# Hybrid decoder layer on one core: alternating head products, adaLN operands swapped, the convolution's first tap on ACT, chunk order at the merge, the second norm shared with POOL

## The chip, the cores and the metric

One Trainium2 chip, one core of it. The metric is the device time of one launch in microseconds. The engines are TensorE (PE in the profile; PEld is its weight load), VectorE (DVE), ScalarE (ACT), GpSimd (POOL) and SyncE (SP, which only issues DMAs here).

## The reference

One layer for a prompt of 1024 tokens and 8 sample sequences of 4 tokens (1056 token columns together), model width 1024:

```
(s1, a1, g1, s2, a2, g2) = silu(c) @ w_ada + b_ada        # 9 conditioning vectors, 6 x 1024 outputs
h = RMSNorm(x) * (1 + a1) + s1
[q | k | v | hc | B | C | ga | gb] = h @ w_in
A: stick-breaking attention, 8 heads x 64, per-head QK RMSNorm, causal; samples also over 2048 cached keys
B: y = B * dwconv3_causal(C * hc)                          # 512 channels, taps w0, w1, w2 and a bias
mix = (sigmoid(ga) * (o_att @ w_att_out) + sigmoid(gb) * (y @ w_conv_out)) @ w_o
x = x + g1 * mix
x = x + g2 * sqrelu_mlp(RMSNorm(x) * (1 + a2) + s2)        # 1024 -> 4096 -> 1024
```

Outputs are the new x, the normalised keys, the values and the last convolution rows, for both groups. All is fp32.

## The kernel before

Tokens lie on the free axis, channels on the partitions. The 1056 columns are cut into 3 chunks of 352 (`c`), channels into blocks of 128 (`b`). Weights come as units of 128x1024 (`u`) through three buffers `raw`; POOL splits each unit into a high and a low fp32r part (`wh`, `wl`, two of each; L523, L525), and a dense product is three fp32r matmuls per 128 rows (hH.wh, hL.wh, hH.wl), 24 of them for one group (one unit, one chunk) into one PSUM bank. A split of unit u waits until the last group of unit u-2 is done, since it takes over its buffers.

The order is written by hand. Stages:

1. `first_units` (L620 to L650): for each of the 8 channel blocks two adaLN units (`ada`, L607: the weight unit is the operand held in the array, the 9 conditioning vectors pass it), then the first 6 groups of q and k advance by one block. DVE makes `mods` (L1060) and from them the block of h (L1072 to L1082).
2. q, k (head norms on ACT), v.
3. The mix, `for k in range(TICKS)`, 51 ticks, the same list on every engine. A tick holds one attention step: `scores` (512 keys or less by 128 queries, two heads), ACT's sigmoid, DVE's keep factors and scan (L1123, L1132), POOL's product (L550), and in the next tick `turn` (transposes, L701), DVE's copies AT (L1162, L1164) and `values` (L712). It also holds one or two dense groups (`DENSE_A`, and `DENSE_B` in the ticks with k % 8 in 0, 1, 3, 4, 6), one page item of the sample attention (L730, L741, L754), and in 32 of the ticks (k % 3 not 0) one adaLN unit. DVE's `convolve` (L1194) runs right after the last chunk of C has been multiplied by hc, ahead of that tick's `turned`.
4. Merge: o_att and y are split in high and low (`split_hi` on ACT, `split_lo` on DVE), then 24 pairs of half groups (ya, yb), block after block, each block in 3 chunks; DVE multiplies by the gates and adds, and makes mixH and mixL.
5. w_o, 24 groups, blocks 0 to 5 in 3 chunks each, then blocks 6 and 7 chunk by chunk. DVE adds to x (`add_wo`), ACT squares, and `rms2` (L802) sums the squares in the middle of the next group.
6. Second norm by chunk: ACT makes the inverse root, then for 8 blocks DVE scales (L1353), ACT makes h2H (L1006), DVE makes h2L (L1330).
7. MLP, 288 groups.

DVE, ACT and POOL each work strictly in program order, so what stands ahead of a waiting instruction holds all that follows.

Of the kernel before, what the change touches and what calls it, by code (L numbers as in the profile page):

```python
# [51 lines left out]
for _n, _w in (("ident", 128), ("headones", 128), ("scanmask", 513), ("trikeys", 128), ("newkeep", 66), ("newvalid", 256),  # L52
               ("selG", 16), ("headrow", 8)):
    TABLES[_n] = (_at, _at + _w)
    _at += _w
# [6 lines left out]
Group = namedtuple("Group", "kind u c bank eng at before")  # L62

# [8 lines left out]
class Plan:  # L72
# [42 lines left out]
    def build(self):  # L115
# [17 lines left out]
        for b in range(DB):  # L133
            for c in range(NCH):
                self.add("ya", self.merge0 + b, c, "d", b5)
                self.add("yb", self.merge0 + b, c, "d", b5)
        self.start("wo")
        for b in range(6):
            for c in range(NCH):
                self.add("wo", self.wo0 + b, c, "d", b5)  # L140
        for c in range(NCH):
            for b in (6, 7):
                self.add("wo", self.wo0 + b, c, "d", b5)
# [20 lines left out]

PLAN = Plan()
# [19 lines left out]
DENSE_A, DENSE_B, ITEM_AT, TURN_AT, ADA_AT = {}, {}, {}, {}, {}  # L185


def ticks():
    g, m, n = MIX0, 0, 16
    end = PLAN.phase["merge"][0]  # L190
    for k in range(TICKS):
# [13 lines left out]
        if k % 3 != 0 and n < 48:  # L205
            ADA_AT[k] = n
            n += 1
# [74 lines left out]
def program(nc, a):  # L282
    ctx = ExitStack()
    with ctx:
# [14 lines left out]
        cT = put("cT", [P, DB, 9], F32)  # L299
# [56 lines left out]
        h2L = inw("h2L", [P, DB, T], F32R, at=W + 4 * DB * T)  # L356
        top[0] = W + 8 * DB * T
# [14 lines left out]
        sz_ps, ada_ps, st_ps, o_ps = bank[2][:, 0:P], bank[3][:, 0:9], bank[4][:, 0:P], bank[6][:, 0:P]  # L372
# [6 lines left out]
        def tb(name, rows=P, lo=0, hi=None):  # L379
# [10 lines left out]
            csig c_ready squares rms_done rstd dense_done bank_dve bank_act dve_step act_step  # L390
# [5 lines left out]
            x1_done squares2 rms2_done rstd2 scaled2 h2_hi h2_lo hid_hi hid_lo y_ready y_out  # L396
# [17 lines left out]
        def _(sp):  # L414
# [59 lines left out]
            def load_x(b):  # L474
                sp.wait_ge(S["mix_lo"], NCH * (5 + b // 2))
                sp.dma_start(act8[:, b, :], a["xT"][:, b, :]).then_inc(S[f"x_in{b}"], 16)
# [26 lines left out]
        def _(pool):  # L503
# [8 lines left out]
            mark(pool.memset(ones[:, :], 1.0))  # L512
            pool.wait_ge(S["pool_step"], steps[0])
# [57 lines left out]
            for u in range(42, len(PLAN.where)):  # L571
                split(u)

        @block.tensor
        def _(pe):
# [62 lines left out]
            for kt in range(DB):  # L638
                for m in (kt, DB + kt):
                    if kt:  # L640
                        pe.wait_ge(S["mods_done"], ADA_NTH[m] - 1)
                    ada(m, bank[6 + m // DB][:, 0:9])
                if kt == 0:
                    pe.wait_ge(S["rstd"], NCH)
                    continue
                first_units(kt - 1)
# [30 lines left out]
            def scores(k):  # L677
                st = STEPS[k]
                for h in (0, 1):
# [5 lines left out]
                    if h == 1 and k - 1 in ADA_AT:  # L685
                        pe.wait_ge(S["mods_done"], ADA_NTH[ADA_AT[k - 1]] + 1)
# [17 lines left out]
            def values(k):  # L704
# [3 lines left out]
                for h in (0, 1):  # L708
                    pe.wait_ge(S["at_out"], 2 * k + h + 1)
                    head = slice((2 * st.p + h) * HD, (2 * st.p + h + 1) * HD)  # L710
# [3 lines left out]
                    mm.then_inc(S["av_done"], 1)  # L714
# [51 lines left out]
            for k in range(TICKS):  # L766
                if k < NSTEP:
                    scores(k)
                if k in DENSE_A:
                    dense(DENSE_A[k], hH, hL)  # L770
                if k in TURN_AT:
# [33 lines left out]
            pe.wait_ge(S["mix_lo"], NCH * DB)  # L805
            pe.wait_ge(S["s_o"], 2)
            for n in range(QK_N):
                dense(WO0 + n, mixH, mixL, halfway=(lambda n=n: rms2(n - 1)) if n else None)

            for g in range(MLP0, len(GROUPS)):  # L810
                if GROUPS[g].kind == "m1":
                    f, q, c = GROUPS[g].c
                    if f == 0:
                        pe.wait_ge(S["h2_lo"], DB * (c + 1) + (c == NCH - 1))
# [5 lines left out]
                          (lambda: rms2(QK_N - 1)) if g == MLP0 else None).then_inc(S["dense_done"], 1)  # L820
# [12 lines left out]
        def _(act):  # L833
# [11 lines left out]
            act.activation(cT[:, :, :].rearrange("p k c -> p (k c)"), sm("cT"), ACT.Sigmoid).then_inc(S["csig"], 1)  # L845
            act.preload_act_table_set("natural_log_exp_and_others")
            act.wait_ge(S["consts"], 1)
# [75 lines left out]
            spills = {}  # L923

            def evict(g, k):
# [5 lines left out]
                elif kind == "gate":  # L931
# [7 lines left out]
                    if c == NCH - 1:  # L939
                        spills[k + 1] = ("gate", n, g)  # L940
                elif kind == "B" and c == NCH - 1:
# [17 lines left out]
            for k in range(TICKS):  # L959
                if k < NSTEP:  # L960
                    probability(k)
                if k in spills:
                    spill(*spills[k])
                if k in DENSE_A:
# [5 lines left out]
                if k == NSTEP + 1:  # L970
                    split_hi(0)
# [3 lines left out]
            split_hi(1)  # L975
# [3 lines left out]
            for n in range(NCH * DB):  # L979
                b, c = n // NCH, n % NCH  # L980
# [11 lines left out]
            def inverse2(c):  # L992
                act.wait_ge(S["rms2_done"], 18 + 2 * c + 2)
# [4 lines left out]
            def second_hi(c):  # L998
                n = CH if c < 2 else LASTP
                if c == 2:  # L1000
                    act.wait_ge(S["scaled2"], 17)
                    act.activation(h2H[:, :, samp], hs2[:, :, :], ACT.Copy).then_inc(S["h2_hi"], 1)
                for b in range(DB):
                    x = DB * c + b
                    act.wait_ge(S["scaled2"], x + 1 + (c == 2))
                    act.activation(h2H[:, b, c * CH:c * CH + n], sc[x % 3][:, 0:n], ACT.Identity, bias=mods[:, 24 + b, 0:1])\  # L1006
                        .then_inc(S["h2_hi"], 1)

            for n in range(18):
                square2(n)  # L1010
            for c in range(NCH):
                square2(18 + 2 * c)
                square2(19 + 2 * c)
                inverse2(c)
                second_hi(c)
# [14 lines left out]
        def _(dve):  # L1030
# [21 lines left out]
            tt(cT[:, :, :], sm("cT").rearrange("p (k c) -> p k c", k=DB), cT[:, :, :], ALU.mult).then_inc(S["c_ready"], 1)  # L1052
# [3 lines left out]

            def modulation(m, ps):
                dve.wait_ge(S["ada_done"], ADA_NTH[m] + 1)
# [7 lines left out]
            for b in range(DB):  # L1066
                for m in (b, DB + b):
# [126 lines left out]
            def convolve(cb):  # L1194
# [4 lines left out]
                if cb:  # L1199
                    dve.wait_ge(S["spill1"], 16 * cb)  # L1200
                own()
                mark(cp(tail[:, cb, 0:2], up[:, 0:2]))
                last = cp(tail[:, cb, 2:18].rearrange("p (b j) -> p b j", j=2), us[:, :, 0:2])
                if cb == CB - 1:
                    last.then_inc(S["tail_ready"], 1)
                else:
                    mark(last)
                mark(ts(y, up[:, 2:SEQ + 2], w(0), sm("conv_b", cb, cb + 1), ALU.mult, ALU.add))
                mark(ts(ys, us[:, :, 2:6], w(0), sm("conv_b", cb, cb + 1), ALU.mult, ALU.add))
                own()  # L1210
                mark(stt(y, up[:, 1:SEQ + 1], w(1), y, ALU.mult, ALU.add))
                mark(stt(ys, us[:, :, 1:5], w(1), ys, ALU.mult, ALU.add))
                own()
                mark(stt(y, up[:, 0:SEQ], w(2), y, ALU.mult, ALU.add))
                mark(stt(ys, us[:, :, 0:4], w(2), ys, ALU.mult, ALU.add))

            def evict(g):
# [3 lines left out]
                if kind == "C":  # L1221
# [9 lines left out]
                    dve.wait_ge(S["bank_dve"], GROUPS[g].at)  # L1231
                    convolve(cb)
                elif kind == "B":
# [253 lines left out]
```

## Time and profile before

| | |
|---|---|
| median of 3 runs | 1870.39 us (1869.11 to 1870.75) |
| the profiled execution | 1871.02 us, its span 1869.2 us |
| PE busy | 1777.9 us, 95% of the span |
| DVE, POOL, ACT busy | 878.6, 659.8, 299.3 us |
| mean granted clock of TensorE | 0.966 |
| PE idle for DVE or ACT at the second norm's sums (L802) | 22.1 us |
| HBM traffic | 104 GB/s over the span |

The median of the runs and the profiled execution differ by 0.6 us. A matmul's own duration (about 320 ns for 352 columns) is longer than the distance to the next one, since they are pipelined; durations of a stretch are therefore read from start to start. The granted clock is a share of TensorE's 2.4 GHz: 1.00 or 0.50 (1.2 GHz) at any moment, in between only as a mean.

### The profile page before, as it was taken

To read this page: it belongs to the slowest core of one execution; us is meant where nothing else is said; L and a number is where in the kernel's file an instruction comes from. 1 tells how busy PE (TensorE), PEld (TensorE's weight loads), DVE (VectorE), ACT (ScalarE), POOL (GpSimd) and SP (SyncE) were. 2 spreads that over 40 slices of the span, in tenths; PEclk is the share of its full clock that TensorE was granted. 3 is DMA by queue.
4 is the path that set the end of the run, shared out by engine and by line. 5 is a ranking of instruction groups with operands and counts; after the bars stand their busy time and mean duration, and the time that the engine had idled before them with its cause. 6 is when DMAs were issued, how large, how long until landed. Compare 5 with 4: busy or idle time off the path is not lost. (4 is left out here: it accounts for less than half of the span.)

```text
span 1869.2 us, 29718 instructions
## 1 busy us (share of the span) xinstructions
PE 1777.9 (95%) x11934; PEld 1657.0 (89%) x11934; DVE 878.6 (47%) x1425; ACT 299.3 (16%) x583; POOL 659.8 (35%) x377
## 2 busy tenths in 40 slices
PE   7999998997989999999898969999999999999999
PEld 6989777776778887879898868999999999999999
DVE  1434155545444444432783246555454545455553
ACT  3123211010101111111210123201020202020200
POOL 1037034343424443442342213433333333333332
PEclk8699999998989999999999989999999999999999
DMA  6312064444544665643432101111111111111112
GB/s 218 118 55 79 35 223 165 155 161 137 196 144 156 227 205 183 212 150 127 186 138 93 45 23 35 46 46 46 46 48 53 47 46 46 46 46 46 46 46 93
DMA packets 72505, 196.83 MB, mean 105 GB/s; under 512 B 8081, under 2 KB 8210, under 8 KB 72370
## 3 DMA queue, kind: packets, MB, share of 16 engines
q1 hardware_dynamic: 67682, 179.76, 28.6%
q10 hardware_dynamic: 4688, 15.18, 2.1%
q8 instruction: 96, 1.57, 0.3%
q14 instruction: 39, 0.32, 0.0%
HBM read 175.41 MB, written 19.50 MB: 104 GB/s over the span
## 5 line engine op out<-in xcount | busy, mean ns | idle before, releaser
L523 POOL TENSOR_TENSOR wh<-raw,zero 128x1024 fp32r<-128x1024 f32 x116 | 220.0, 1897 | 789.0 <-PE bank L589 700.3
L525 POOL TENSOR_TENSOR wl<-raw,wh 128x1024 fp32r<-128x1024 f32 x116 | 285.2, 2458 | 9.1
L589 PE MATMUL bank<-hH,wh 128*128 128x352 f32 x816 | 280.5, 344 | 3.0 <-POOL wl L525 3.0
L589 PE MATMUL bank<-hL,wh 128*128 128x352 f32 x816 | 266.5, 327 | 0.0
L589 PE MATMUL bank<-hH,wl 128*128 128x352 f32 x816 | 266.0, 326 | 0.0
L589 PE MATMUL bank<-h2H,wh 128*128 128x352 f32 x768 | 248.4, 323 | 0.9 <-issue 0.9
L1303 DVE SCALAR_TENSOR_TENSOR act<-bank,mods,act 128x352 f32<-128x352 f32 (+1 forms) x216 | 122.3, 571 | 268.0 <-PE bank L589 262.0
L589 PE MATMUL bank<-hidH,wh 128*128 128x352 f32 x768 | 247.7, 323 | 0.0
L589 PE MATMUL bank<-h2H,wl 128*128 128x352 f32 x768 | 246.3, 321 | 0.0
L550 POOL TENSOR_TENSOR beta<-beta,kb 128x512 f32<-128x512 f32 (+3 forms) x96 | 122.5, 1296 | 350.9 <-DVE kb L1132 350.9
L589 PE MATMUL bank<-hidH,wl 128*128 128x352 f32 x768 | 246.3, 321 | 0.0
L589 PE MATMUL bank<-h2L,wh 128*128 128x352 f32 x768 | 246.1, 320 | 0.0
L589 PE MATMUL bank<-hidL,wh 128*128 128x352 f32 x768 | 246.1, 320 | 0.0
L589 PEld LDWEIGHTS bank<-hH,wh 128*128 128x128 f32 x816 | 156.9, 192 | 33.2 <-issue 25.8
L1371 DVE TENSOR_TENSOR rsq<-rel 128x352 f32<-128x352 f32 x96 | 92.1, 959 | 165.3 <-ACT rel L1024 165.3
L589 PEld LDWEIGHTS bank<-hH,wl 128*128 128x128 f32 x816 | 157.5, 193 | 1.8
L589 PEld LDWEIGHTS bank<-hL,wh 128*128 128x128 f32 x816 | 156.7, 192 | 0.0
L589 PEld LDWEIGHTS bank<-h2H,wh 128*128 128x128 f32 x768 | 144.3, 188 | 1.2 <-issue 1.1
L589 PEld LDWEIGHTS bank<-h2H,wl 128*128 128x128 f32 x768 | 144.6, 188 | 0.1
L589 PEld LDWEIGHTS bank<-hidH,wl 128*128 128x128 f32 x768 | 144.3, 188 | 0.0
L589 PEld LDWEIGHTS bank<-hidH,wh 128*128 128x128 f32 x768 | 144.1, 188 | 0.0
L589 PEld LDWEIGHTS bank<-h2L,wh 128*128 128x128 f32 x768 | 144.1, 188 | 0.0
(147 smaller groups left out, 2667.9 us busy)
## 6 DMA issues: line engine op xcount, KB each, us to landing
raw<-in_weights SPq DMA_DIRECT2D x168, 512.0 KB, 3.6
ring<-in_cache_k SPq DMA_DIRECT2D x128, 256.0 KB, 4.0
ring<-in_cache_v SPq DMA_DIRECT2D x128, 256.0 KB, 3.6
gate_scratch<-gt ACTq DMA_DIRECT2D x16, 528.0 KB, 3.7
act<-gate_scratch SPq DMA_DIRECT2D x16, 528.0 KB, 4.5
xt<-in_xT SPq DMA_DIRECT2D x8, 528.0 KB, 9.0
act<-in_xT SPq DMA_DIRECT2D x8, 528.0 KB, 4.5
out_yT<-act SPq DMA_DIRECT2D x8, 528.0 KB, 2.7
```

Source lines behind the costliest of these rows:

```text
L523: mark(pool.tensor_tensor(wh[u % 2][:, :], src[:, :], zero[:, 0:1].to_broadcast([P, 1024]), ALU.add))
L525: pool.tensor_tensor(wl[u % 2][:, :], src[:, :], wh[u % 2][:, :].bitcast(F32), ALU.subtract)\
L550: pool.tensor_tensor(b[:, 1:st.n + 1], b[:, 1:st.n + 1], kb[x % 4][:, 0:st.n], ALU.mult)\
L589: mm = pe.matmul(out, x, y, start=n == 0, stop=n == end)
L1303: one = stt(x, ps[:, 0:CH if c < 2 else LASTP], mods[:, col, 0:1], x, ALU.mult, ALU.add)
L1371: mark(tt(rsq[x % 2][:, :], rel[x % 2][:, :], rel[x % 2][:, :], ALU.mult))
```

## The change

- `values`: the products of the two heads of a step (each writes 64 partitions of the same bank) alternate, and both wait for the second head's AT.
- adaLN: the 9 vectors, padded to 32 columns, are held in a quarter of the array's columns (four quarters for 8 blocks of rows), and the weight unit passes them. The partial sums (4 x 32 rows x 128) go through a DVE copy `ada_y` and a second small product with `sel9`, which adds the quarters and turns the result. In the mix this turn stands one tick later; in stage 1 it stands behind the preceding block's 18 dense products.
- Convolution: tap 0 and bias go to ACT (`conv_first`); taps 1 and 2 stay on DVE but move to the first chunk of B, and where that is a `DENSE_A` group, behind `turned`.
- `split_hi` of chunks 0 and 1 one and two ticks earlier. The last two blocks of the merge go chunk by chunk, as do the first two of w_o, and the first w_o groups wait only for their own chunk of mixL.
- Second norm: of chunks 0 and 2, blocks 5 to 7 are scaled and subtracted on POOL, with two ACT operations each between; all of w_o's last four additions stand together ahead of chunk 1; the sums of groups 20 to 23 are taken later.

```diff
+MERGE_ORDER = by_blocks(range(6)) + by_chunks((6, 7))
+WO_ORDER = by_chunks((0, 1)) + by_blocks(range(2, 6)) + by_chunks((6, 7))
...
             def ada(m, out):
                 for kt in range(DB):
-                    mm = pe.matmul(out, raw[i % NRAW][:, kt * P:(kt + 1) * P], cT[:, kt, :], start=kt == 0, stop=kt == DB - 1)
+                    at = 32 * (kt % 4)
+                    mm = pe.matmul(out[at:at + 32, :], cT[:, kt, :], raw[i % NRAW][:, kt * P:(kt + 1) * P],
+                                   start=kt < 4, stop=kt >= 4, tile_position=(0, at))
                 mm.then_inc(S["ada_done"], 1)
+
+            def ada_turn(m, out):
+                n = ADA_NTH[m]
+                pe.wait_ge(S["ada_copied"], n + 1)
+                pe.matmul(out[:, 0:9], ada_y[n % 2][:, :], tb("sel9"), start=True, stop=True).then_inc(S["ada_turned"], 1)
...
             def values(k):
-                for h in (0, 1):
-                    pe.wait_ge(S["at_out"], 2 * k + h + 1)
-                    for j in range(st.n // P):
+                pe.wait_ge(S["at_out"], 2 * k + 2)
+                for j in range(st.n // P):
+                    for h in (0, 1):
...
+            def second_scaled(c):        # POOL
+                pool.wait_ge(S["rstd2"], c + 1)
+                pool.wait_ge(S["x1_done"], 20 + 2 * c)
+                for b in (5, 6, 7):
+                    pool.tensor_tensor(h2f[:, b, cols], act8[:, b, cols], rst2[:, cols], ALU.mult)
+                for b in (5, 6, 7):
+                    pool.wait_ge(S["p_hi"], (3 if c else 0) + b - 4)
+                    pool.tensor_tensor(h2L[:, b, cols], h2f[:, b, cols], h2H[:, b, cols].bitcast(F32), ALU.subtract)
...
+            second_scaled(0)
+            split(PLAN.mlp0)
+            split(PLAN.mlp0 + 1)
+            second_scaled(2)
...
+                for x in {21: (), 22: (), 23: (20, 21)}.get(n, (n - 1,) if n else ()):
+                    rms2(x)
...
+            inverse2(0)                  # ACT
+            second_hi(0, range(2))
+            second_pool(0)
+            second_hi(0, range(2, 5))
...
-                mark(ts(y, up[:, 2:SEQ + 2], w(0), sm("conv_b", cb, cb + 1), ALU.mult, ALU.add))
-                mark(ts(ys, us[:, :, 2:6], w(0), sm("conv_b", cb, cb + 1), ALU.mult, ALU.add))
+                dve.wait_ge(S["conv_first"], 2 * cb + 2)
...
+            for n in range(20):          # DVE
+                add_wo(n)
+            second_norm(0)
+            for n in range(20, 24):
+                add_wo(n)
+            second_norm(1)
+            second_norm(2)
```

PE, stage 1, between the dense products of one channel block and the next. Before (the two adaLN units of the next block, 9 columns per product, then the dense products):

```order
L632 MATMUL bank<-hL,wh_63 128x352
L611 MATMUL bank<-cT,raw_59 128x9 [waits raw_in0,mods_done]
L611 MATMUL bank<-cT,raw_59 128x9 x7
L611 MATMUL bank<-cT,raw_60 128x9 [waits raw_in1,mods_done]
L611 MATMUL bank<-cT,raw_60 128x9 x7
L630 MATMUL bank<-hH,wh_62 128x352 [waits h_sample,h_lo]
```

and now:

```order
L677 MATMUL bank<-hL,wh_65 128x352
L657 MATMUL bank<-tables,ada_y_54 128x9 [waits ada_copied]
L657 MATMUL bank<-tables,ada_y_55 128x9 [waits ada_copied]
L650 MATMUL bank<-raw_61,cT 32x128 [waits raw_in0,mods_done]
L650 MATMUL bank<-raw_61,cT 32x128 x7
L650 MATMUL bank<-raw_62,cT 32x128 [waits raw_in1,mods_done]
L650 MATMUL bank<-raw_62,cT 32x128 x7
L675 MATMUL bank<-hH,wh_64 128x352 [waits h_sample,h_lo]
```

The turns of a block's two units now stand behind the dense products of the block before it, and the dense products that follow need the block of h which DVE makes from these turns.

DVE, the mix, tick 3: C's last chunk is taken (`up`, `us`), the convolution `gt`, the copies AT, B's first chunk. Before:

```order
L1228 TENSOR_TENSOR up<-bank,gt_90 128x320
L1229 TENSOR_TENSOR us<-bank,gt_90 128x8x4
L1202 COPY tail<-up 128x2 [waits dve_step,bank_dve]
L1203 COPY tail<-us 128x16
L1208 TENSOR_SCALAR gt_91<-up,small 128x1024
L1209 TENSOR_SCALAR gt_91<-us,small 128x32
L1211 SCALAR_TENSOR_TENSOR gt_91<-up,small,gt_91 128x1024 [waits dve_step]
L1212 SCALAR_TENSOR_TENSOR gt_91<-us,small,gt_91 128x32
L1214 SCALAR_TENSOR_TENSOR gt_91<-up,small,gt_91 128x1024 [waits dve_step]
L1215 SCALAR_TENSOR_TENSOR gt_91<-us,small,gt_91 128x32
L1162 TENSOR_TENSOR AT_78<-bank,tables 128x128 [waits av_done,at_done]
```

and now:

```order
L1333 TENSOR_TENSOR us<-bank,gt_92 128x8x4
L1171 TENSOR_SCALAR mods<-bank,small 128x9 [waits ada_turned]
L1271 TENSOR_TENSOR AT_80<-bank,tables 128x128 [waits av_done,at_done]
L1273 COPY AT_80<-bank 128x384
L1271 TENSOR_TENSOR AT_81<-bank,tables 128x128 [waits av_done,at_done]
L1273 COPY AT_81<-bank 128x384
L1309 SCALAR_TENSOR_TENSOR gt_93<-up,small,gt_93 128x1024 [waits conv_first,bank_dve]
L1310 SCALAR_TENSOR_TENSOR gt_93<-us,small,gt_93 128x32
L1311 COPY tail<-up 128x2
L1313 SCALAR_TENSOR_TENSOR gt_93<-up,small,gt_93 128x1024 [waits dve_step]
L1314 SCALAR_TENSOR_TENSOR gt_93<-us,small,gt_93 128x32
```

The copies AT, for which PE's `values` waits, no longer stand behind the convolution.

POOL, around the first two units of the MLP (each a `wh` and a `wl` row). Before the splits followed each other directly; now:

```order
L595 TENSOR_TENSOR h2f<-act_68,rst_123 128x352 [waits x1_done,rstd2]
L595 TENSOR_TENSOR h2f<-act_68,rst_123 128x352 x2
L599 TENSOR_TENSOR h2L<-h2f,h2H 128x352 [waits p_hi] x3
L541 TENSOR_TENSOR wh_64<-raw_63,zero 128x1024 [waits raw_in2,dense_done]
L543 TENSOR_TENSOR wl_66<-raw_63,wh_64 128x1024 [waits pool_step]
L541 TENSOR_TENSOR wh_65<-raw_61,zero 128x1024 [waits raw_in0,dense_done]
L543 TENSOR_TENSOR wl_67<-raw_61,wh_65 128x1024 [waits pool_step]
L595 TENSOR_TENSOR h2f<-act_68,rst_123 128x320 [waits x1_done,rstd2]
```

Six operations of the norm stand ahead of the first split of the MLP, and six more behind the second.

## Rows read from the trace of the kernel before

**Rows 1.** Windows: stretch, length, busy PE PEld DVE ACT POOL, clock, DMA, GB/s.

```profile
27.39:102.75 75.36, 72.35 (x400) 72.06 (x400) 32.20 (x70) 13.02 (x23) 4.28 (x3) 0.71 0.37 119
238.70:887.50 648.80, 610.39 (x4983) 522.90 (x4984) 306.77 (x606) 94.27 (x192) 252.36 (x184) 0.97 0.52 176
1089.48:1154.02 64.54, 46.63 (x250) 43.84 (x248) 40.62 (x71) 24.20 (x46) 12.41 (x6) 0.84 0.05 17
1154.02:1869.20 715.18, 710.15 (x4465) 709.89 (x4464) 360.13 (x503) 87.66 (x182) 267.93 (x123) 1.00 0.15 50
```

**Rows 2.** Waits of PE: who waited for whom, total us, times, longest.

```profile
PE bank L802 <- ACT sq L990: 22.1, 9, 10.8
PE bank L712 <- DVE AT L1164: 16.8, 9, 4.8
PE bank L701 <- DVE sAT L1175: 9.5, 2, 9.1
...
PE bank L688 <- DVE mods L1064: 8.7, 2, 4.5
PE bank L589 <- DVE mixL L1287: 5.4, 1, 5.4
PE bank L589 <- DVE act L1279: 4.0, 1, 4.0
...
PE bank L589 <- DVE oyL L1244: 2.2, 1, 2.2
```

**Rows 3.** Timeline, stage 1, one block: start, length, engine, line, count, idle.

```profile
42.28 4.19 PE L611 MATMUL bank<-cT,raw 128*128 128x9 f32 x32
...
46.51 0.28 DVE L1062 TENSOR_SCALAR mods<-bank,b,small 128x9 f32<-128x9 f32 x1 [2.12 <-PE bank L611]
...
50.61 0.19 DVE L1082 TENSOR_TENSOR hL<-hs,hH 128x32 fp32r<-128x32 f32 x1
```

**Rows 4.** Timeline, a tick of the mix without a second dense group.

```profile
313.34 1.08 PE L730 MATMUL bank<-ring,qb 128*32 128x128 f32 x32
314.36 1.09 PE L701 MATMUL bank<-tables,beta 128*128 128x128 f32 x8
315.29 1.85 PE L611 MATMUL bank<-cT,raw 128*128 128x9 f32 x16
...
316.40 0.55 DVE L1164 COPY AT<-bank 128x384 f32<-128x384 f32 x1
...
317.07 1.58 PE L712 MATMUL bank<-AT,vsb 128*64 128x128 f32 x16
318.58 1.06 PE L754 MATMUL bank<-ring,sAT 128*32 128x512 f32 x8
```

**Rows 5.** Timeline, PE, a step with one key block per head.

```profile
352.36 0.44 PE L712 MATMUL bank<-AT,vsb 128*64 128x128 f32 x4
352.73 1.06 PE L754 MATMUL bank<-ring,sAT 128*32 128x512 f32 x8
```

**Rows 6.** Lines by form, PEld: the weight loads of the sample scores.

```profile
L730 PEld LDWEIGHTS bank<-ring,qb 128*32 128x32 f32 x1024 | 26.0, 109 | 7.1 <-issue 7.1
```

**Rows 7.** Timeline, DVE, in the first convolution.

```profile
284.82 2.34 DVE L1209 TENSOR_SCALAR gt<-us,small 128x32 f32<-128x32 f32 x1
```

**Rows 8.** Windows behind the first and the last of the convolution's four stalls.

```profile
290.94:294.30 3.36, 3.36 (x18) 2.96 (x20) 0.95 (x3) 0.00 (x0) 0.00 (x0) 0.50 0.00 0
...
516.05:523.00 6.95, 6.95 (x19) 5.45 (x20) 2.87 (x4) 0.69 (x1) 2.65 (x2) 0.51 0.02 7
```

**Rows 9.** Timeline, DVE, first chunk of the second norm, first and last operation.

```profile
1093.05 1.08 DVE L1353 SCALAR_TENSOR_TENSOR sc<-act,mods,rst 128x352 f32<-128x352 f32 x2 [2.98 <-ACT rst L996]
...
1100.99 0.58 DVE L1330 SCALAR_TENSOR_TENSOR h2L<-sc,mods,h2H 128x352 fp32r<-128x352 f32 x1 [0.16 <-ACT h2H L1006]
```

**Rows 10.** The page, costliest groups: POOL's two-input operations.

```profile
L525 POOL TENSOR_TENSOR wl<-raw,wh 128x1024 fp32r<-128x1024 f32 x116 | 285.2, 2458 | 9.1
L550 POOL TENSOR_TENSOR beta<-beta,kb 128x512 f32<-128x512 f32 (+3 forms) x96 | 122.5, 1296 | 350.9 <-DVE kb L1132 350.9
```

More of the change, by code:

```diff
@@ L62, with by_chunks, by_blocks @@
 Group = namedtuple("Group", "kind u c bank eng at before")
+def by_chunks(blocks):
+    return [(b, c) for c in range(NCH) for b in blocks]
+def by_blocks(blocks):
+    return [(b, c) for b in blocks for c in range(NCH)]
+MERGE_ORDER = by_blocks(range(6)) + by_chunks((6, 7))
+WO_ORDER = by_chunks((0, 1)) + by_blocks(range(2, 6)) + by_chunks((6, 7))
 def mlp_order():
@@ L162, in free_at @@
         return self.end[before] if before >= 0 else 0
+SC_NTH = {}
+for _c in range(NCH):
+    for _b in range(DB if _c == 1 else 5):
+        SC_NTH[_c, _b] = len(SC_NTH)
+SC_SLOT = {_x: _n % 3 for _x, _n in SC_NTH.items()}
 PLAN = Plan()
@@ L206, in ticks @@
             ADA_AT[k] = n
+            ADA_TURN_AT[k + 1] = n
             n += 1
@@ L1009, in _, with second_hi @@
-            for n in range(18):
-                square2(n)
[L1011 to L1015, printed above, removed]
+            seen = [0]
+            def second_hi(c, blocks):
+                for b in blocks:
+                    seen[0] += 1
+                    act.wait_ge(S["scaled2"], seen[0])
+                    if b is None:
+                        act.activation(h2H[:, :, samp], hs2[:, :, :], ACT.Copy).then_inc(S["h2_hi"], 1)
+                        continue
+                    n = CH if c < 2 else LASTP
+                    act.activation(h2H[:, b, c * CH:c * CH + n], sc[SC_SLOT[c, b]][:, 0:n], ACT.Identity,
+                                   bias=mods[:, 24 + b, 0:1]).then_inc(S["h2_hi"], 1)
@@ new lines, in second_pool @@
+            def second_pool(c):
+                cols = slice(c * CH, c * CH + (CH if c < 2 else LASTP))
+                for b in (5, 6, 7):
+                    x = h2f[:, b, cols]
+                    act.wait_ge(S["p_scaled"], (3 if c else 0) + b - 4)
+                    mark(act.activation(x, x, ACT.Identity, scale=mods[:, 32 + b, 0:1], bias=mods[:, 24 + b, 0:1]))
+                    own()
+                    act.activation(h2H[:, b, cols], x, ACT.Copy).then_inc(S["p_hi"], 1)
+            for n in range(20):
+                square2(n)
@@ L1017, in _ @@
+            inverse2(0)
+            second_hi(0, range(2))
+            second_pool(0)
+            second_hi(0, range(2, 5))
+            for n in (20, 21, 22):
+                square2(n)
+            inverse2(1)
+            square2(23)
+            second_hi(1, range(5))
+            inverse2(2)
+            second_hi(1, range(5, DB))
+            second_hi(2, (None, 0, 1))
+            second_pool(2)
+            second_hi(2, range(2, 5))
             x = 0
@@ L1066, in _ @@
             for b in range(DB):
+                for m in (b, DB + b):
+                    ada_copy(m, bank[6 + m // DB][:, 0:P])
                 for m in (b, DB + b):
@@ L1249, in _ @@
                     keep_and_scan(k)
-                if k in DENSE_A:
+                late = k in DENSE_A and GROUPS[DENSE_A[k]].kind == "B" and GROUPS[DENSE_A[k]].c == 0
+                if k in DENSE_A and not late:
                     evict(DENSE_A[k])
+                if k in ADA_TURN_AT:
+                    modulation(ADA_TURN_AT[k], ada_ps[:, 0:9])
                 if k in TURN_AT:
@@ L1257, in _ @@
                     turned(k - 1)
+                if late:
+                    evict(DENSE_A[k])
                 if k in DENSE_B:
```

187 lines of the change are left out of this document (106 added, 81 removed).

## The prediction, on record before the changed kernel ran

> **What bounds the kernel now.** I read the windows by stage first [rows 1]: in the mix PE is busy for 610 of 649 us, DVE for 307, POOL for 252, ACT for 94. So what shortens PE's stream or its waits shortens the kernel, and the rest counts only where PE waits for it. The MLP (715.2 us) is 4465 matmuls in 710.2 us, 0.159 us each at clock 1.00, so a group of 24 is 3.82 us, and the change leaves it alone. Stage 1 runs at a mean clock of 0.71, and the second norm uses 64.5 us with 46.6 us of PE in it. The waits of PE [rows 2] name the rest: the norm's sums, AT, sAT and mods in the mix, and single waits at the entries of the merge (4.0 and 2.2) and of w_o (5.4).
>
> **Stage 1: +3 us (bounds -8 and +13).** Before, two adaLN units take 4.2 us of PE [rows 3] between 18 dense products, and DVE prepares the block behind them, so PE never idles; but these products of 9 columns pull the clock to 0.50, and the mean is 0.71 [rows 1]. Now the turns stand behind the preceding block's dense products, and the next dense products need the block of h made from these turns: a chain that closes every round. One round is the 18 products (2.9 us at 2.4 GHz, double that, 5.3, at 1.2 by these rows' spacing with some overlap), about 0.65 us for the turns, and DVE's 4.3 us from the last mods to the last hL (46.51 to 50.80) [rows 3]: 7.8 to 10.4 us, against 75.4/8 = 9.4 before. PE idles about 3 us per round, so the clock can fall here as before. I take 9.2 us, seven rounds, about 7 us until the first block is ready (two products, copies and turns 2.5, then 4.3), 4.2 us for the last dense products and the same 3 us wait for POOL's split at the end: 78.6 us, +3. All rounds fast give 67.5, all slow 88.
>
> **The ticks of the mix: -28 us (bounds -15 and -45).**
> - adaLN unit: 16 instructions hold PE from 315.29 to 317.07, 1.78 us [rows 4]. The nearest row to the new form is the sample scores, also 32 held columns and 128 passing ones in four quarters: 32 instructions from 313.34 to 314.36, 1.02 us [rows 4]. Half is 0.51, with a change of tiling on entry I take 0.65: 1.13 saved. The turn is two instructions of 9 columns, 0.22 by the spacing of 1.78/16, with its entry 0.3, in 32 ticks +9.6.
> - values: a step of four key blocks per head takes 1.51 us (317.07 to 318.58) [rows 4], one of a single block per head, where the heads alternate by themselves, 0.37 for 4 instructions [rows 5]. If some 0.15 of both is the change to the next tiling, a pair costs 0.22, and four pairs 1.03: 0.48 saved, for fewer blocks less, 0.3 on average.
> - Where it counts: values waits for AT. In the 30 ticks with a second dense group (3.8 us between turn and values) AT is long ready; 20 of them have an adaLN unit: 20 x 1.13 + 30 x 0.3 = 31.6. In 12 ticks only the adaLN unit stands in between. In the tick shown AT is ready at 316.95 and values began at 317.07: PE will now wait for AT, and ends at 316.95 + 1.03 = 317.98 rather than 318.58, 0.6 saved, 12 x 0.5 = 6. In the 6 bare ticks values waits already, and now for the second head: nothing. So 31.6 + 6 - 9.6 = 28.
> - The lower bound takes nothing from alternation and 0.9 for a unit; the upper all of 32 x 1.13 and 48 x 0.3 against turns at 0.15.
>
> Here a rule speaks against the change. The trace puts 32 loads and products of quarter width into 1.02 us, 32 ns a pair, though one load alone is shown with 109 ns [rows 4, 6]; so loads and products in neighbouring columns do overlap. The Trainium skill (TensorE: Matmul & The Clock Gate, Part 3: Packing small matmuls) says that weight loads overlap running matmuls only when the row group differs, which column tiles do not. By that rule an adaLN unit would take several us; the trace does not agree. It is kept as the last rival.
>
> **The convolution: -31 us (bounds -36 and -15).** It sits ahead of turned, sample_turned and evictions on DVE, and four of PE's waits are its: 4.8 (AT), 9.1 (sAT), 4.5 and 4.2 (mods, 8.7 in two) [rows 2], 22.6 us. Behind them the clock is at 0.50 for 22.5 us of running products (first and last of four stretches in [rows 8]), which costs half, 11.2. Part of the length is POOL: a 32-column tap took 2.34 us [rows 7]. With tap 0 on ACT and the rest behind turned, what is left on DVE (two taps, about 3.5 us, or up to 8 with POOL's splits between) lies beside PE's second dense group, adaLN unit, values and sample values, about 6.5 us, before anything waits for it. In tick 14 an ada_copy stands behind it, for which the next scores wait; I leave 3 us for that: 33.8 - 3 = 31.
>
> That 2.34 us for 32 columns ends with a POOL operation of 2.5 us [rows 7, 10]. The Trainium skill (SBUF — State Buffer, Who interferes with whom) says why: VectorE with two SBUF inputs or in a two-port mode and GpSimd exclude each other for whole instructions. The trace agrees. The rule speaks against the norm's move to POOL below, where both engines work on SBUF at once.
>
> **Entry of the merge: -7 us (bounds -10 and -3).** The waits for oyL and for the gated product, 2.2 + 4.0 [rows 2], both come from split_hi issued late: gates are loaded only when all of split_lo is done. Two chunks earlier brings the end of split_lo forward by some 4 us; about 1.8 us of waiting for the gates stay, and some 2.5 us of slow clock behind the wait go. **Entry of w_o: -6 us (bounds -8 and 0).** The 5.4 us wait for the last mixL goes [rows 2], with 2 us of slow clock; but the splits of w_o's first two units (4.3 us each: a wl of 2.5 [rows 10] and a somewhat shorter wh) now have one group of 3.82 before them, 0.7 each.
>
> **Second norm: -12 us (bounds -25 and 0).** Before, 64.5 us hold ten groups (38.2) and five sums of 0.5, so 23.8 are lost to waiting (6.9 and 10.8 at the sums) and slow clock. After, counted from the end of group 19: its sum and the inverse root are ready at 3.7. DVE's 8 blocks took 1093.05 to 1101.57, 8.5 us, one block about 1.0 [rows 9]. Now 5 blocks are on DVE, but ACT has 11 operations of 0.6 in a fixed order, with the three of POOL in the middle, and a POOL operation of 352 columns costs about 1.2 us by L550's 1296 ns [rows 10] and excludes DVE's: chunk 0 ends at 14, not earlier than before. What is gained is that groups 20 to 22 run meanwhile without waiting for sums. Group 23 waits about 2 us for sums 20 and 21 and ends at 18.1. The first MLP groups end at 26.3. Chunk 1 is all on DVE, from 19, beside POOL's split of 4.3 us, and ends at 31: 4.7 us of idle. Chunk 2 ends at 41 against 38.6: 2.6. That is 9.3 idle and, with 3 for the clock, 12.3 against 23.8: -11.5, taken as 12.
>
> **Sum.** 3 - 28 - 31 - 7 - 6 - 12 = -81 us. The profiled execution took 1871.0 us, the median is 1870.4: 1790 us for the median.
>
> **Rivals.**
> - More is gained: stage 1 keeps the full clock in most rounds (-8 instead of +3), and the gaps of the mix no longer lower the clock, another 8 to 10. For: the narrow products are shorter. Against: PE idles 3 us per round in stage 1. 1770 us. Chance 0.17.
> - The convolution's stall moves rather than goes: ada_copy, the B eviction or the next keep factors wait behind it while POOL splits, in all four places some 4 us and the slow clock with it. For: POOL can stretch its 3.5 us to 8. Against: 6.5 us of PE's work lie before it. Half of the 31 stays: 1806 us. Chance 0.14.
> - The norm gains nothing since POOL and DVE exclude each other and ACT's order adds: chunks 1 and 2 late by 6 us each: 1802 us. Chance 0.12.
> - Slower: products in neighbouring column quarters take turns with their loads. A pair then costs 109 ns of load [rows 6] and the 107 ns of a full-width one, 16 pairs 3.46 us against 1.78: the 32 units of the mix cost +54 instead of -23 - 6, and stage 1's 16 at least another 8. 1790 + 83 + 8 = 1881. It decides from about 3.4 us per unit on. Against: 32 such pairs in 1.02 us [rows 4]. Chance 0.03, in which I include what I don't see.
> - The forecast case, 0.54, with its own range 1778 to 1802.
>
> **Range and chances.** 1766 to 1828: it takes in the first three rivals and the sum of several lower bounds, and leaves out less than 0.2. What can be told from no change is 0.2%, 3.7 us: faster 0.96, within 0.01, slower 0.03.
>
> **What would show it.** In the new profile: an adaLN unit's 16 instructions in 0.5 to 0.7 us; values of four blocks in about 1.0 us; waits of PE for AT about 1 us in each of 12 ticks and not over 5 us anywhere near a convolution; stage 1 of 67 to 88 us with PE idle about 3 us per block, waiting for hL; no wait of 5 us before w_o; and a stretch of 50 to 56 us from group 19 to the sixth MLP group. I am wrong if the mix stays above 610 us, if the wait behind the convolution only changes its line, or if the norm's chunk 1 ends later than 35 us after group 19.

## The result and the profile after

The changed kernel takes 1797.41 us (median of 4 runs, 1793.89 to 1801.87) against 1869.89 for the kernel before on the same chip: a ratio of 0.962, with a 95% interval of 0.960 to 0.9641. On a second chip it took 1794.17 us, ratio 0.960 (0.9581 to 0.9619). Its profiled execution took 1793.89 us, with a span of 1792.1 and a mean clock of 0.979.

The windows by stage of the changed kernel, columns as in [rows 1]: stage 1, the mix, the stretch from the end of w_o's group 19 to the sixth MLP group, and the rest.

```profile
26.82:110.72 83.90, 54.68 (x433) 51.17 (x433) 35.92 (x86) 12.28 (x21) 4.29 (x3) 0.69 0.32 107
246.65:830.13 583.48, 550.84 (x5046) 455.62 (x5047) 308.25 (x632) 102.91 (x202) 254.09 (x184) 0.99 0.58 196
1025.14:1076.74 51.60, 44.81 (x250) 42.22 (x248) 40.00 (x59) 26.38 (x52) 25.75 (x18) 0.93 0.07 21
1076.74:1792.10 715.36, 710.14 (x4464) 709.89 (x4464) 360.13 (x503) 87.69 (x182) 268.14 (x123) 1.00 0.16 50
```

Against [rows 1], the mix is 65 us shorter (648.8 to 583.5), 60 of them PE's busy time. Stage 1 is 8.5 us longer although PE is busy 18 us less in it. The norm's stretch goes from 64.5 to 51.6, and the MLP is unchanged.

The waits of PE, columns as in [rows 2]:

```profile
PE bank L761 <- DVE AT L1273: 27.5, 18, 4.1
PE bank L675 <- DVE hL L1191: 24.2, 7, 4.5
...
PE bank L855 <- ACT sq L1068: 6.1, 7, 2.0
PE bank L626 <- POOL wl L543: 4.9, 4, 2.0
PE bank L626 <- DVE h2L L1443: 4.7, 1, 4.7
PE bank L626 <- DVE act L1389: 3.4, 1, 3.4
```

The sums now cost 6.1 us of waiting where they cost 22.1; the mods, and the oyL and mixL, are gone from the list. Waiting for AT has grown from 16.8 to 27.5 us, since units and values are shorter and PE meets DVE earlier. Waiting for hL is new, and it is stage 1's.

One round of stage 1 in the timeline, PE and DVE (start, length, instruction, count, idle before):

```profile
62.38 0.63 PE L675 MATMUL bank<-hH,wh 128*128 128x352 f32 x1 [3.29 <-DVE hL L1191]
...
67.63 0.51 PE L657 MATMUL bank<-tables,ada_y 128*128 128x9 f32 x4
68.23 1.08 PE L650 MATMUL bank<-raw,cT 128*32 128x128 f32 x32
72.60 0.63 PE L675 MATMUL bank<-hH,wh 128*128 128x352 f32 x1 [3.29 <-DVE hL L1191]
...
67.95 0.23 DVE L1171 TENSOR_SCALAR mods<-bank,small 128x9 f32<-128x9 f32 x1 [5.32 <-PE bank L657]
```

A round takes 10.22 us: 5.25 of dense products, 0.6 of turns, 1.1 of units and 3.29 of idle time. The dense products run at half clock (0.29 us from start to start, against 0.16 at full). DVE stands idle for 5.32 us, waiting for turns that are queued on PE behind those slow products; then PE waits for what DVE makes of them.

A tick of the mix as in [rows 4], on PE:

```profile
312.96 1.09 PE L750 MATMUL bank<-tables,beta 128*128 128x128 f32 x8
313.98 0.64 PE L650 MATMUL bank<-raw,cT 128*32 128x128 f32 x16
315.71 1.09 PE L761 MATMUL bank<-AT,vsb 128*64 128x128 f32 x16 [1.08 <-DVE AT L1273]
316.73 1.06 PE L804 MATMUL bank<-ring,sAT 128*32 128x512 f32 x8
```

The unit holds PE for 0.65 us (1.78 before), then PE waits 1.08 us for AT, then values takes 1.02 (1.51 before). From the start of the unit to the end of values it is 2.75 us against 3.29.

### The profile page after: what moved, and what is told of

Same layout as the page of the kernel before. It is cut to its first block, busy times and chain, and to the rows that moved or that the text cites. A ratio compares the mean times of both kernels' runs of the same rounds, so it can differ in the third digit from the quotient of the medians.

```text
span 1792.1 us, 30076 instructions
## 1 busy us (share of the span) xinstructions
PE 1697.5 (95%) x12030; PEld 1565.8 (87%) x12030; DVE 879.7 (49%) x1453; ACT 307.7 (17%) x597; POOL 675.6 (38%) x390
## 4 chain that ended last, share of the span: by engine, by line
PE 89%; DVE 5%; issue 2%; ACT 2%; POOL 1%; DMA 1%; ACTq 0%; SPq 0%; DVEq 0%; POOLq 0%
PE bank L626 73%; PE bank L737 2%; PE bank L761 2%; PE bank L804 2%; PE bank L780 2%; PE bank L750 1%; PE bank L663 1%; PE bank L675 1%; PE bank L855 1%; DVE AT L1273 1%; PE bank L702 1%; PE bank L650 1%; PE bank L676 1%; PE bank L677 1%; POOL wl L543 1%
## 5 line engine op out<-in xcount | busy, mean ns | idle before, releaser
L626 PE MATMUL bank<-hH,wh 128*128 128x352 f32 x816 | 276.7, 339 | 2.0 <-POOL wl L543 2.0
L626 PE MATMUL bank<-hL,wh 128*128 128x352 f32 x816 | 262.9, 322 | 0.0
```

The costliest lines, as they stand in the source:

```text
L626: mm = pe.matmul(out, x, y, start=n == 0, stop=n == end)
```

## The experiments

Each was timed against the kernel before on the same chip; the chips differ from one group of runs to the next.

**One part at a time.** Four kernels, each the kernel before with one part of the change (of each diff only the telling lines): the order of heads in `values`; the adaLN operands, `ada_y` and turns; tap 0 on ACT with the later place of the convolution; and all from the merge on.

```diff
 # values alone
-                for h in (0, 1):
-                    pe.wait_ge(S["at_out"], 2 * k + h + 1)
-                    for j in range(st.n // P):
+                pe.wait_ge(S["at_out"], 2 * k + 2)
+                for j in range(st.n // P):
+                    for h in (0, 1):
 # adaLN alone
-                    mm = pe.matmul(out, raw[i % NRAW][:, kt * P:(kt + 1) * P], cT[:, kt, :], ...)
+                    mm = pe.matmul(out[at:at + 32, :], cT[:, kt, :], raw[i % NRAW][:, kt * P:(kt + 1) * P], ...)
 # convolution alone
+                if k in firsts:
+                    convolve_first(*firsts.pop(k))
 # tail alone
+MERGE_ORDER = by_blocks(range(6)) + by_chunks((6, 7))
+WO_ORDER = by_chunks((0, 1)) + by_blocks(range(2, 6)) + by_chunks((6, 7))
```

> The kernel before with the alternating heads alone. Theory A (the parts add up and each works as its rows say): four pairs take 1.02 us instead of 1.51, three 0.81 instead of 1.08, fewer nothing; this counts in the 42 ticks where a dense group or an adaLN unit covers AT, about 12 us in all, so 1858 us, with the waits for AT in the bare ticks growing by some 0.6 us each. Rival B (alternation matters only because it goes with the shorter adaLN units): no change, 1867 to 1873 us.

> The kernel before with the swapped adaLN operands alone, turns and all. Theory A: 32 units of the mix go from 1.78 to 0.58 us plus a turn of 0.14, 20 of them count in full and 12 for some 0.7, about 29 us; stage 1 gets longer by the chain through DVE, 75.4 to 84 us; in all 1850 us. Rival B (the clock: units of full activity keep TensorE at 2.4 GHz in stage 1 and in the mix): stage 1 shorter than 75 us and 1835 us or less.

> The kernel before with the convolution's change alone (tap 0 on ACT, the rest at B's first chunk, late). Theory A: the four stalls of 4.8, 4.5, 9.1 and 4.2 us go and the slow clock behind them (11 us): 33 us less, 1837 us, and no wait of PE over 5 us in the mix. Rival B (the stall moves to another wait): 1850 us or more with new waits of 3 us or more at the four places.

> The kernel before with the change of everything behind the mix alone: split_hi earlier, chunk order of merge and w_o, second norm with POOL. Theory A: entry of the merge and waits there 1 to 3 us, entry of w_o 5 us, from w_o's start to the sixth MLP group 14 us: 20 us less, 1850 us. Rival B (this part owes its gain to the phase of the clock, not to the order): less than 12 us, 1858 us or more.

| kernel | median us | ratio (95%) | stage 1 | mix | merge to sixth MLP group |
|---|---|---|---|---|---|
| before | 1868.26 | | 75.4 | 648.6 | 266.7 |
| values alone | 1860.37 | 0.9959 (0.9947 to 0.9971) | 73.9 | 641.0 | 266.7 |
| adaLN alone | 1857.72 | 0.9939 (0.9922 to 0.9955) | 85.8 | 626.3 | 266.1 |
| convolution alone | 1835.70 | 0.9826 (0.9809 to 0.9842) | 75.4 | 614.8 | 265.1 |
| tail alone | 1849.62 | 0.9898 (0.9882 to 0.9915) | 75.4 | 649.3 | 245.5 |
| all | | | 83.9 | 583.5 | 246.6 |

(The last three columns are from each one's profiled execution.) The four gains are 7.9, 10.5, 32.6 and 18.6 us, 69.6 together against the 72.5 of the whole change (75.6 on the second chip), so they nearly add. The convolution and the tail came out as the first theory had it, within 1.5 us. Values alone gained 7.9 us of the 12 that it gave: PE's waiting in the mix grew from 38.8 to 46.0 us, 6.5 of it for AT, and the time at half clock from 44.4 to 51.2. (Its stage 1, which the edit doesn't touch, is 1.5 us shorter; so much can differ from one execution to the next.) AdaLN alone was 8 us slower than the first theory said, and its stage 1 of 85.8 us rules out the second: its mix gained 22.3 us, and the waiting in the mix grew there from 38.8 to 47.2 us, 6.0 of it for AT. The four stalls behind the old convolution stay, 24.9 us against 22.6; the last of them, 5.3 us, is now for the DVE copy `ada_y`. Convolution alone takes the waiting in the mix from 38.8 to 16.9 us and the time at half clock from 44.4 to 20.5 us. Half of the latter difference is 11.9, and 21.9 + 11.9 is just the 33.8 us that its mix is shorter.

**The changed kernel again**, as the baseline of the next three.

> The changed kernel once more, as the yardstick for the next runs on one chip. Theory A: 1794 to 1802 us, as its four runs so far; where a run is at the upper end, the trace shows the same stages and more slow clock in the mix.

It took 1794.17 us (1793.86 to 1796.19). The profiled execution is the slowest of the four, with a stage 1 of 85.8 us, a mix of 585.2 with 10.2 us at half clock (6.8 in the first profile), and 245.1 from the merge to the sixth MLP group.

**The second norm without POOL.** All 8 blocks of chunks 0 and 2 are DVE's; the order of chunks, sums and additions stays.

```diff
-            second_scaled(0)
-            second_scaled(2)
...
-                blocks = range(DB) if c == 1 else range(5)
+                blocks = range(DB)
```

> The changed kernel with all 8 blocks of the second norm on DVE again in every chunk; the order (groups 20 to 23 before the second chunk) stays. Theory A (the order gains, POOL's share does not, since POOL and DVE exclude each other and ACT's fixed order takes what is left): within 2 us of the changed kernel. Rival B (POOL's share is the gain): 6 us or more slower, with the wait for chunk 1 or chunk 0 of the MLP longer by that.

1794.29 us, ratio 0.9597 (0.9576 to 0.9618): no difference in the whole, but from w_o to the sixth MLP group it is 142.3 us against 146.0 to 146.3. In the profiled execution the mix, which the edit doesn't touch, took 589.0 us with 20.5 us at half clock, and that hides the 4 us there. It doesn't explain the equal medians, since the mean clocks of the four runs are alike (0.977 to 0.981 against 0.977 to 0.980). The groups by line on DVE from 1025 to 1080 us, first the changed kernel (count | busy, mean ns | idle before):

```profile
L1468 DVE SCALAR_TENSOR_TENSOR sc<-act,mods,rst 128x352 f32<-128x352 f32 (+1 forms) x18 | 14.9, 838 | 3.0 <-ACT rst L1074 3.0
L1443 DVE SCALAR_TENSOR_TENSOR h2L<-sc,mods,h2H 128x352 fp32r<-128x352 f32 (+1 forms) x18 | 13.9, 778 | 3.8 <-ACT h2H L1087 3.7
```

and without POOL's share:

```profile
L1462 DVE SCALAR_TENSOR_TENSOR sc<-act,mods,rst 128x352 f32<-128x352 f32 (+1 forms) x24 | 15.5, 656 | 3.0 <-ACT rst L1071 3.0
L1437 DVE SCALAR_TENSOR_TENSOR h2L<-sc,mods,h2H 128x352 fp32r<-128x352 f32 (+1 forms) x24 | 13.6, 568 | 1.0 <-ACT h2H L1084 0.8
```

36 operations beside POOL keep DVE busy for 28.8 us, and 48 of them without POOL's share for 29.1. What POOL took over saved DVE nothing, and PE's wait for chunk 1 is 3.38 us in place of 4.69:

```profile
1059.48 0.43 PE L624 MATMUL bank<-h2H,wh 128*128 128x352 f32 x1 [3.38 <-DVE h2L L1437]
```

So the shorter stretch comes from the order of chunks and sums; POOL's share takes back about 4 us of it, of which the clock may be a part (3.4 us at half clock behind group 19 here, 6.8 with POOL's share).

**Tap 0 back on DVE, in the new place.**

```diff
-                if k in firsts:                             # ACT, at two places
-                    convolve_first(*firsts.pop(k))
...                                                         # DVE
-                dve.wait_ge(S["conv_first"], 2 * cb + 2)
...
+                mark(ts(y, up[:, 2:SEQ + 2], w(0), sm("conv_b", cb, cb + 1), ALU.mult, ALU.add))
+                mark(ts(ys, us[:, :, 2:6], w(0), sm("conv_b", cb, cb + 1), ALU.mult, ALU.add))
```

> The changed kernel with tap 0 and bias of the convolution back on DVE, at the new late place. Theory A (the place matters, not the tap): 0 to 4 us slower, no wait over 3 us at the four places. Rival B (the tap on DVE, blocked by POOL, was the stall): 10 us slower or more.

1805.04 us (1800.60 to 1807.84), ratio 0.965 (0.9627 to 0.9674), 10.9 us more than the changed kernel, just over the 10 us of the rival. But the rival's reason is not there: PE waits for AT as long as before, 27.5 us. The traces don't place all of the 10.9. The mix is 593.9 us against 583.5 and 585.2, with 36.3 us of waiting against 33.1 and 33.2, but 23.9 us at half clock against 6.8 and 10.2; and 3.5 us come from w_o on, where the edit touches nothing. So about 3 us are waits, perhaps 7 the clock, and what sets the extra slow stretches is open. One trace alone would not tie them to the tap, since the run without POOL's share had 20.5 us at half clock in an unedited mix; but the mean clocks of all four runs are low (0.973 to 0.977, against 0.977 to 0.980 on the same chip).

**The convolution back in its old place, tap 0 still on ACT.**

```diff
-                    firsts[k if DENSE_A.get(k) == g else k + 1] = ((u - 12) // 3, g)
+                    convolve_first((u - 12) // 3, g)
...                                                         # DVE, after C's last chunk
+                    dve.wait_ge(S["bank_dve"], GROUPS[g].at)
+                    convolve(cb)
...
-                late = k in DENSE_A and GROUPS[DENSE_A[k]].kind == "B" and GROUPS[DENSE_A[k]].c == 0
+                late = False
```

The last two lines also take B's first chunk ahead of `turned` again, as in the kernel before.

> The changed kernel with the convolution back at C's last chunk, ahead of the copies AT, but with tap 0 on ACT. Theory A (the place matters): 12 us slower or more, with four waits of 2 to 6 us again and slow clock behind them. Rival B (the tap matters): 5 us or less.

1834.87 us, ratio 0.9819 (0.98 to 0.9838), 40.7 us more than the changed kernel. Its timeline on PE, at the four convolutions:

```profile
298.47 1.97 PE L761 MATMUL bank<-AT,vsb 128*64 128x128 f32 x16 [4.66 <-DVE AT L1269]
...
364.30 1.61 PE L737 MATMUL bank<-act 64*128 64x384 f32 x2 [4.80 <-issue]
...
441.66 1.94 PE L750 MATMUL bank<-tables,beta 128*128 128x128 f32 x8 [8.30 <-DVE sAT L1280]
...
513.99 2.04 PE L737 MATMUL bank<-act 64*128 64x512 f32 x2 [4.97 <-DVE ada_y L1158]
```

These are 22.7 us of waiting, where [rows 2] has 22.6 at the same four places: with a tap less on DVE nothing of it is saved. DVE spends the time waiting for ACT's tap, and for POOL. In the first of them, on DVE, with POOL's split:

```profile
291.33 1.62 DVE L1305 SCALAR_TENSOR_TENSOR gt<-up,small,gt 128x1024 f32<-128x1024 f32 x1 [1.69 <-ACT gt L996]
292.88 2.35 DVE L1306 SCALAR_TENSOR_TENSOR gt<-us,small,gt 128x32 f32<-128x32 f32 x1
...
297.12 0.55 DVE L1269 COPY AT<-bank 128x384 f32<-128x384 f32 x1
...
291.95 3.23 POOL L543 TENSOR_TENSOR wl<-raw,wh 128x1024 fp32r<-128x1024 f32 x1
```

In the changed kernel the same two operations stand behind the copies, and so does POOL's hold on the 32-column one:

```profile
289.40 0.55 DVE L1273 COPY AT<-bank 128x384 f32<-128x384 f32 x1
290.18 1.62 DVE L1309 SCALAR_TENSOR_TENSOR gt<-up,small,gt 128x1024 f32<-128x1024 f32 x1 [0.23 <-ACT gt L996]
291.72 2.35 DVE L1310 SCALAR_TENSOR_TENSOR gt<-us,small,gt 128x32 f32<-128x32 f32 x1
...
290.80 3.24 POOL L543 TENSOR_TENSOR wl<-raw,wh 128x1024 fp32r<-128x1024 f32 x1
```

Both times the 32-column operation ends within 0.05 us of POOL's. The convolution is not shorter there; it is late for nobody. What its place is worth is shown with the tap on ACT; the early place with the tap on DVE was not run in the changed kernel.

**Stage 1, turns ahead of the dense products of the block before.** This breaks the loop that the round above shows.

```diff
                 if kt == 0:
                     pe.wait_ge(S["rstd"], NCH)
-                else:
-                    first_units(kt - 1)
                 for m in (kt, DB + kt):
                     ada_turn(m, bank[6 + m // DB])
+                if kt:
+                    first_units(kt - 1)
```

> The changed kernel with one thing other in stage 1: the turns of a block stand on PE ahead of the preceding block's 18 dense products instead of behind them, so DVE makes the next block while PE multiplies. Theory A (the chain through the turns is what made stage 1 longer, and its idle holds the clock down): a round goes from 10.2 us to DVE's own 5.7 (copies 0.5, turns 0.3, mods 0.5, block 4.3), the clock stays up, stage 1 from 84 to about 50 us, 1764 us. Rival B (the clock stays low, since PE still waits in each round): rounds of 8 us, stage 1 about 66 us, 1780 us.

1766.68 us (1763.01 to 1771.04), ratio 0.9464 (0.9444 to 0.9483): some 28 us faster than the changed kernel, near the first theory's 1764 us. Stage 1 takes 51.8 us. Its windows from 46 to 77.6 us, and its timeline on PE and DVE:

```profile
46.00:77.60 31.60, 25.15 (x256) 22.66 (x256) 22.96 (x55) 7.32 (x12) 3.93 (x2) 0.99 0.48 167
```

```profile
59.89 1.08 PE L650 MATMUL bank<-raw,cT 128*32 128x128 f32 x32
61.55 0.61 PE L657 MATMUL bank<-tables,ada_y 128*128 128x9 f32 x4 [0.58 <-DVE ada_y L1162]
62.02 0.41 PE L675 MATMUL bank<-hH,wh 128*128 128x352 f32 x1
...
65.07 1.08 PE L650 MATMUL bank<-raw,cT 128*32 128x128 f32 x32
66.75 0.61 PE L657 MATMUL bank<-tables,ada_y 128*128 128x9 f32 x4 [0.59 <-DVE ada_y L1162]
...
61.21 0.48 DVE L1162 COPY ada_y<-bank 128x128 f32<-128x128 f32 x2
61.98 0.23 DVE L1171 TENSOR_SCALAR mods<-bank,small 128x9 f32<-128x9 f32 x1 [0.28 <-PE bank L657]
```

A round is 5.2 us, at a clock of 0.99: DVE works on the next block while PE does the dense products, and PE idles 0.6 us in a round rather than 3.3. DVE's own chain now sets the round: in it DVE waits only 0.28 us for a turn and 0.67 for ACT. Two things went at once, since with the short gaps the clock stayed up: of the 5.0 us a round, 2.2 are in the dense products (5.25 to 3.05) and 2.7 in the gap. What each would give without the other is not shown.

**The same with the copies of the next units earlier on DVE**, between a block's scaling and its hL, to take away the 0.6 us.

```diff
-                for m in (b, DB + b):
-                    ada_copy(m, bank[6 + m // DB][:, 0:P])
...
+                if b < DB - 1:
+                    for m in (b + 1, DB + b + 1):
+                        ada_copy(m, bank[6 + m // DB][:, 0:P])
```

> As the run before, and DVE's two copies for the next block's turns stand in the gap in which DVE waits for ACT's hH. Theory A: the copies and the wait for the turns leave DVE's chain, a round is 5.0 us, stage 1 about 45 us, 5 us less than the run before. Rival B (PE or the loading of the weight units sets the round, 1 MB in 5 us): no gain over the run before, with PE waiting for raw.

1770.66 us (1768.51 to 1775.69), ratio 0.9486 (0.9465 to 0.9507): no gain, and stage 1 at 56.9 us is 5 us longer. The timeline, DVE and PE:

```profile
64.43 0.73 DVE L1162 COPY ada_y<-bank 128x128 f32<-128x128 f32 x2 [1.62 <-PE bank L650]
65.07 1.27 DVE L1192 SCALAR_TENSOR_TENSOR hL<-xt,mods,hH 128x1024 fp32r<-128x1024 f32 x1
...
66.60 0.40 PE L675 MATMUL bank<-hH,wh 128*128 128x352 f32 x1 [1.00 <-DVE hL L1194]
```

The copies now wait 1.62 us for units that stand on PE behind the dense products, and hold hL back, for which PE then waits 1.00: a round of 5.92 us. The gap was closed at one end and opened at the other. It is no gain, as the second theory had it, but for another reason: PE waits for hL, not for raw.

**Turns first and the norm without POOL**, together.

> The changed kernel with two edits at once: in stage 1 PE turns a block's two adaLN units before the dense products of the block before it, and the second norm's 8 blocks are all made by DVE. Turning first alone gave 1766.7 us, with a stage 1 of 51.8 us against 83.9 and rounds of 5.2 us. The norm on DVE alone gave 1794.3, the same time, though its stretch from w_o to the sixth MLP group took 142.3 us against 146.3. Theory A: the norm's 4 us are real and were lost by chance to slow clock in the mix (20.4 us of it against 6.8, where nothing was edited): 1763 us, range 1760 to 1767. Rival B: the norm is worth nothing and the two stretches only trade with the clock: 1767 us or more, up to 1772.

1760.52 us (median of 6 runs), ratio 0.9431 (0.9417 to 0.9445), in the first theory's range. Five of the runs lie between 1758.08 and 1764.40, with a median of 1759.60; one took 5430.84 us, which nothing here explains, and it is not in the ratio. Stage 1 is 50.8 us and the norm's stretch again 142.3. It is the fastest version measured, 6 us below turns first alone, on another chip and with intervals that just touch. Its mean clocks are higher as well (0.987 to 0.993 in the five runs, against 0.985 to 0.988 with turns first alone), so how much of the 6 us is the norm's is open.

## Why the prediction was right, and where its terms were off

1790 us was forecast, 1797.4 measured. The medians differ by 72.5 us, and the profiled executions by 77.1, where the sum was 81; the profiled execution is the fastest of the changed kernel's four. The terms, each from the two profiled executions:

| term | forecast | measured |
|---|---|---|
| stage 1 | +3 | +8.5 |
| ticks | -28 | -31.3 (65.1, less the convolution's; alone values gave 7.6 and adaLN 22.3) |
| convolution | -31 | -33.8 (alone) |
| entry of the merge | -7 | -1.6 |
| entry of w_o | -6 | -5.6 |
| second norm | -12 | -12.9 |

The total is near partly by luck: two misses of some 5.5 us each at the cost of the change stand against one of 6 in its favour.

**Stage 1** is the term with the largest miss. Seven rounds were forecast at 9.2 us, between 7.8 (full clock) and 10.4 (half). The start-up (6.3 us, forecast 7) and the end (7.4, forecast 7.2) were right, and the seven rounds took 70.1 us, 10.0 each, which is the slow end: five took 10.20 to 10.24, with nearly all their dense products at half clock, and the first two 9.5, with two thirds. (A slow round's parts, 5.3 + 0.65 + 4.3, add to 10.25, not to the 10.4 of the prediction.) Five other profiled executions with this stage 1 took 84.2 to 85.8 us, so the +8.5 is the low end. The prediction had the reason in hand, a PE idle for 3 us in every round, and still took a value between the two. It also took the order as given: it called the chain one "that closes every round", but did not ask whether the turns have to stand where they do. The run with turns first shows that the place costs 32 us of stage 1, against the 8.5 that the change shows there.

**Ticks.** A unit measured 0.58 us (forecast 0.65), a turn 0.14 (0.3), values of four, three and two blocks per head 1.02, 0.81 and 0.59 (forecast 1.03 for four; before 1.51, 1.08, 0.60). The turn was the mis-sized one: over 32 ticks 0.16 us each, 5 us. The waits for AT came as forecast, 1.08 us in the tick of [rows 4], with the 0.6 us saved there as 0.54. The rival in which neighbouring column quarters take turns is out: 16 loads and products in 0.58 us are 36 ns a pair.

**Convolution.** The place works as the prediction said, in all four ticks; the 3 us left over for a late `ada_copy` were not needed. The early place brings back the 22.7 us of waits. That ACT's tap matters was not separately priced; it is worth 11 us in the medians, for the most part not as waiting, and why is open.

**Entry of the merge.** Two steps failed. The timeline, DVE and PE:

```profile
833.16 4.62 DVE L1349 TENSOR_TENSOR oyL<-act,oyH 128x1408 fp32r<-128x1408 f32 x2 [5.30 <-ACT oyH L1031]
842.54 0.95 DVE L1389 TENSOR_TENSOR act<-bank,act 128x352 f32<-128x352 f32 x2 [4.77 <-DMA act<-gate_scratch]
...
843.21 0.63 PE L626 MATMUL bank<-oyH,wh 128*128 128x352 f32 x1 [3.38 <-DVE act L1389]
```

The last oyL is done at 837.78, 7.7 us into the merge; before it was 898.05, 10.7 us in. That is 3 us and not 4, and PE itself comes 2.15 us sooner, since its wait for oyL is gone; so the gated product, with the gates' 4.8 us of DMA in front of it, is waited for 3.4 us and not 1.8. The stretch at half clock behind that wait stayed as long (6.8 us), and a wait of 0.83 us for POOL's split is new. The clock's part of this is chance: of the eight other profiled executions with this merge, in this kernel and its variants, seven have 3.4 us at half clock and take 97.9 to 98.3 us for it, against 99.3 here; with the tail alone the merge is 2.9 us shorter than before.

**Entry of w_o.** The 5.43 us wait is now 1.03 for POOL's split, and 0.5 behind it; these are the 0.7 each that were forecast.

**Second norm.** The waits came where they were put, on PE:

```profile
1041.01 1.69 PE L855 MATMUL bank<-sq,ones 128*128 128x352 f32 x4 [1.99 <-ACT sq L1068]
...
1058.56 0.66 PE L626 MATMUL bank<-h2H,wh 128*128 128x352 f32 x1 [4.69 <-DVE h2L L1443]
...
1077.75 0.40 PE L626 MATMUL bank<-h2H,wh 128*128 128x352 f32 x1 [1.01 <-POOL wl L543]
```

Forecast were 2 at the sums, 4.7 at chunk 1 and 2.6 at chunk 2; the last is not there, only 1 us for a split just behind the sixth group. That 4.7 came out so exactly is luck in part: chunk 1 was ready 33.4 us after group 19, not 31, and PE came to it at 28.7, not 26.3. The rival "the norm gains nothing" was wrong on the stretch and right that POOL's share costs: the run on DVE alone shows that it takes about 4 us back. The Trainium skill (SBUF — State Buffer, Who interferes with whom) says that a VectorE instruction with two SBUF inputs and a GpSimd instruction that reads SBUF contend for one port pair, which the first to start holds to its end. The mean DVE operation of 838 ns beside POOL, against 656 without its share, agrees.

## What to carry to other kernels

In a pipelined loop over blocks, write the small product that starts the other engines' chain ahead of the long products that don't need it: behind them it closes a loop in which each engine waits for the other once per round, and the idle time can bring the slow clock too (here 10.2 us a round against 5.2). Work on a busy in-order engine that nobody waits for soon goes behind what is waited for soon: here that took away 22 us of waits, while the version shortened by a tap waited as long as ever in the old place. Its length is not free in the new place either; the tap back on DVE cost 3 us of waits and 10.9 in all. Before a vector engine's work is shared with a neighbour on the same memory, compare its busy time with and without: a quarter fewer operations left DVE as busy as before.

## What the runs showed of the hardware

- Loads and products of neighbouring column tiles overlap: 16 pairs of 32 held columns and 128 passing ones take 0.58 us, 36 ns a pair, where one load alone is recorded with 109 ns [rows 6]; 16 with 128 held and 9 passing took 1.78. With 64 held columns the two halves alternating take 1.02 us for 16, and one after the other 1.51.
- Waiting alone doesn't tell what a stall costs. In the convolution-alone run 21.9 us of waits went, and 33.8 of time; the rest is half of the time that the clock no longer spends at 1.2 GHz. This count is rough: for the convolution back in its old place it gives 21.9 + 23.9 = 45.8 us, and the mix is 39.6 longer.
- DVE and POOL on SBUF at once: in the norm 838 and 778 ns a DVE operation against 656 and 568 without POOL's share, and 2.35 us for one of 32 columns in the convolution, ending with POOL's split.
